# The projections of the mixed input as 16 column pairs of 7 block products each, with staging through DRAM and other fillers in the attention

## The reference

```python
h = rmsnorm(x, norm_mix_g)
proj = h @ w_in                                   # 1024 x 4104
u_pool, q, k, v, f_logit, g_logit = jnp.split(proj, IN_SPLITS, axis=-1)   # 512, 512, 512, 512, 8, 2048
y_pool = pool_mixer(u_pool, pool_w, pool_scale) @ w_pool_out
y_fox = forgetting_attention(q, k, v, f_logit + b_forget) @ w_fox_out     # 8 heads of 64
gates = jax.nn.sigmoid(g_logit + b_gate)
g_pool, g_fox = gates[..., :D], gates[..., D:]
x = x + (g_pool * y_pool + g_fox * y_fox) @ w_out
```

```python
x = x + memory_cross_attention(rmsnorm(x, norm_x_g), rmsnorm(mem, norm_mem_g), w_xq, w_xkv, w_xo)
gu = rmsnorm(x, norm_ffn_g) @ w_ffn_in
x = x + (jax.nn.silu(gu[..., :D_FF]) * gu[..., D_FF:]) @ w_ffn_out
return rmsnorm(x, norm_final_g)
```

## Time and profile before

| | |
|---|---|
| median of 3 runs | 1522.72 us |
| profiled execution | 1521.78 us, of which the span is 1519.9 us |
| PE (matmul) | 1466.1 us busy, 96% of the span |
| DVE | 898.3 us, 59% |
| ACT | 555.7 us, 37% |
| POOL | 377.9 us, 25% |
| DMA | 147.79 MB moved |

### The profile page before, as it was taken

The page is one execution under the profiler, slowest core; times in us unless marked ns, Lnnn a source line. Parts: engine busy times, 40 slices in busy tenths (PEclk is TensorE's granted clock), DMA queues, the critical chain, the costliest instruction groups (busy, mean ns, idle before and its releaser), DMA issues.

```text
span 1519.9 us, 18589 instructions
## 1 busy us (share of the span) xinstructions
PE 1466.1 (96%) x7268; PEld 1211.3 (80%) x7268; DVE 898.3 (59%) x1226; ACT 555.7 (37%) x987; POOL 377.9 (25%) x311
## 2 busy tenths in 40 slices
PE   5999999999999999999999799999999999999996
PEld 5778888788787888888877678888888888887785
DVE  4272522566665423327563866777677776878966
ACT  5224311656654322216451542222222222444344
POOL 4000000000000000105001654444444443448203
PEclk9999999999999999999999899999999999999998
DMA  7333355531110352513210223323332224883333
GB/s 183 54 48 56 72 82 83 98 57 22 49 29 29 73 80 83 222 51 105 67 42 28 111 70 104 105 104 104 104 104 104 104 104 152 304 285 84 104 97 132
DMA packets 103399, 147.79 MB, mean 97 GB/s; under 512 B 4744, under 2 KB 69768, under 8 KB 101904
## 3 DMA queue, kind: packets, MB, share of 16 engines
q1 hardware_dynamic: 94288, 117.72, 30.0%
q0 software_dynamic: 4464, 15.77, 2.9%
q10 hardware_dynamic: 4560, 13.11, 2.2%
HBM read 113.78 MB, written 32.80 MB: 96 GB/s over the span
## 4 chain that ended last, share of the span: by engine, by line
PE 89%; DVE 5%; POOL 2%; DMA 2%; ACT 1%; issue 1%; SPq 0%; POOLq 0%; DVEq 0%; ACTq 0%
PE ps L1553 27%; PE ps L1554 27%; PE ps L1555 27%; PE ps L1803 2%; PE ps L1752 2%; PE ps L1783 1%; DMA w_raw<-in_w_in 1%; DVE t_lo L1054 1%; PE ps L1784 1%; DVE s_lo L1054 1%; POOL w_lo L517 1%; POOL rstd L509 0%; PE ps L1560 0%; PE ps L1995 0%; DVE hf_lo_B L1054 0%
## 5 line engine op out<-in xcount | busy, mean ns | idle before, releaser
L1043 DVE TENSOR_TENSOR w_lo<-w_raw,w_hi 128x1024 fp32r<-128x1024 f32 (+1 forms) x58 | 70.5, 1216 | 232.2 <-ACT w_hi L657 230.3
L1553 PE MATMUL ps<-h_lo,w_hi 128*128 128x512 f32 (+1 forms) x456 | 181.3, 398 | 6.5 <-POOL w_lo L517 4.6
L1555 PE MATMUL ps<-h_hi,w_lo 128*128 128x512 f32 (+1 forms) x456 | 176.8, 388 | 0.0
L1554 PE MATMUL ps<-h_hi,w_hi 128*128 128x512 f32 (+1 forms) x456 | 176.5, 387 | 0.0
L657 ACT ACTIVATE w_hi<-w_raw 128x1024 fp32r<-128x1024 f32 (+1 forms) x66 | 69.4, 1051 | 286.4 <-PE ps L1555 270.7
L1553 PE MATMUL ps<-t_lo,s_hi 128*128 128x512 f32 x308 | 120.2, 390 | 2.3 <-DVE t_lo L1054 1.5
L1555 PE MATMUL ps<-t_hi,s_lo 128*128 128x512 f32 x308 | 119.9, 389 | 0.0
L1554 PE MATMUL ps<-t_hi,s_hi 128*128 128x512 f32 x308 | 119.9, 389 | 0.0
L1553 PEld LDWEIGHTS ps<-h_lo,w_hi 128*128 128x128 f32 x456 | 86.4, 190 | 23.3 <-POOL w_lo L517 4.8
L1555 PEld LDWEIGHTS ps<-h_hi,w_lo 128*128 128x128 f32 x456 | 86.3, 189 | 17.8
L1554 PEld LDWEIGHTS ps<-h_hi,w_hi 128*128 128x128 f32 x456 | 86.6, 190 | 15.5
(11 more groups left out here) (303 smaller groups left out, 3658.8 us busy)
## 6 DMA issues: line engine op xcount, KB each, us to landing
...
```

The source lines that it names most:

```text
L1043: nc.vector.tensor_tensor(w_lo[n % SLOTS][:, 0:w], w_raw[n % RAWS][:, 0:w], w_hi[n % SLOTS][:, 0:w].bitcast(FP32), ALU.subtract).then_inc( ...
L1553: nc.tensor.matmul(dst, w_h, x_l, start=start, stop=False)
L1554: nc.tensor.matmul(dst, w_h, x_h, start=False, stop=False)
L1555: return nc.tensor.matmul(dst, w_l, x_h, start=False, stop=stop)
```

## The change

The 32 column chunks of w_in with 48 matmuls each become 16 column pairs (`PAIR_COL`), each computed by seven products of 12 matmuls, the same scheme as in the FFN. `ORDER1` lists the 112 products: the pairs are, in order, the four pairs of pool gates (0 to 3), the first pair of fox gates, the two of u, two more of fox gates, the two of V, q and k of heads 0 to 3, q and k of heads 4 to 7, and the last pair of fox gates. POOL makes four weight sums for each pair (`front_sum`) and, between those of pair 0 and of pair 1, sixteen sums of the token tiles. The transposes of x are cut into 28 units of four (`front_unit`): the blocks of x for P1 and P2, and then x22, T3, T1, T2 and T4. V is computed with features on the partitions like the rest and transposed back by PE. Results go from one single buffer per block (`c_st`) to DRAM where they are gates, q or k of pairs 1 to 3 or pooled input (d), and are loaded again when they are wanted. The last pair's products P7, P4, P5 and P3 (`DEFER`), the mix, and w_pool_out are the fillers of the attention (`beside`); the q and k of the next pair are no longer computed there, but loaded, rounded and split. The fox output has no gate products left, and reads its gates from DRAM.

On POOL at the start, before: tiles 4 to 7 need four rstds (ms, rstd), and between them stand the last weight splits.

The diff, cut to its core:

```diff
+NF = 16
+PAIR_COL = ([COL_G + 2 * P * i for i in range(4)] + [COL_G + D, 0, 2 * P, COL_G + D + 2 * P, COL_G + D + 4 * P]
+            + [COL_V, COL_V + 2 * P, COL_Q, COL_K, COL_Q + 2 * P, COL_K + 2 * P, COL_G + D + 6 * P])
+GATE_OF = {0: 0, 1: 2, 2: 4, 3: 6, 4: 8, 7: 10, 8: 12, 15: 14}
+U_PAIRS, V_PAIRS, QK0, QK_REST = (5, 6), (9, 10), (11, 12), (13, 14)
+LAST_PAIR = NF - 1
...
+STEADY = (P1, P2, P3, P6, P5, P7, P4)
+STAGE = ([(0, P1), (0, P2), (1, P1), (1, P2)] + [(0, q) for q in (P3, P5, P6, P7, P4)]
+         + [(1, q) for q in (P3, P6, P5, P7, P4)]
+         + [(g, q) for g in range(2, LAST_PAIR) for q in STEADY] + [(LAST_PAIR, q) for q in (P1, P2, P6)])
+DEFER = (P7, P4, P5, P3)
+ORDER1 = STAGE + [(LAST_PAIR, q) for q in DEFER]
...
+RING1 = 6
+LEAD1 = 4
...
+UNITS_AFTER = {0: (8, 9), 1: (10, 11), 2: (12, 13), 3: (14, 15), 4: (16, 17), 5: (18, 19), 6: (20, 21, 22, 23), 7: (24, 25, 26, 27)}
+UNITS_FOR = {P1: 8, P2: 8, P3: 13, P5: 16, P6: 20, P7: 24, P4: 28}
+SPLIT_AT = {2: 0, 6: 1, 9: 2, 13: 3, 17: 4, 21: 5, 25: 6, 29: 7}
...
+            def front_sum(g, i):
...
+                if i == 0:
+                    for half in range(2):
+                        pool.wait_ge(pair_in[g % 2][half], 16 * (g // 2 + 1))
+                    if g:
+                        pool.wait_ge(op_lo, NTH1[g - 1, P7] + 1)
...
+                if i == 3:
+                    nc.gpsimd.tensor_tensor(s1, s2, a11, ALU.add).then_inc(s_sum, 1)
...
+            for t in range(4, T):
+                front_sum(0, t - 4)
+                rstd_of(t)
+            for t in range(4):
+                pool.wait_ge(xn_ready, 4 + t + 1)
+                nc.gpsimd.tensor_tensor(tok_f[:, t, :], x_t[4 + t][:, 0:HALF], x_t[t][:, 0:HALF], ALU.subtract).then_inc(t_sum, 1)
+            nc.gpsimd.memset(f_w[:, :, HEADS:F_ROWS].bitcast(FP32), 0.0).then_inc(consts_set, 1)
+            for t in range(4):
+                pool.wait_ge(unit_done, 12 + t + 1)
+                nc.gpsimd.tensor_tensor(tok_f[:, t, :], x_t[4 + t][:, HALF:], tok_f[:, t, :], ALU.subtract).then_inc(t_sum, 1)
+            for t in range(4):
+                nc.gpsimd.tensor_tensor(x_t[4 + t][:, 0:HALF], x_t[4 + t][:, HALF:], x_t[4 + t][:, 0:HALF], ALU.subtract).then_inc(t_sum, 1)
+            for t in range(4):
+                pool.wait_ge(unit_done, 16 + t + 1)
+                nc.gpsimd.tensor_tensor(tok_f[:, t, :], tok_f[:, t, :], x_t[t][:, HALF:], ALU.subtract).then_inc(t_sum, 1)
...
+            def front_hi_of(n):
+                g, q = ORDER1[n]
+                if n >= RING1:
+                    act.wait_ge(prod_done, n - RING1 + 1)
...
+                    act.wait_ge(s_sum, 4 * g + {P7: 1, P6: 2, P3: 3, P5: 4}[q])
+                nc.scalar.activation(by_k(front_hi[n % RING1]), front_operand(g, q), ACT.Copy).then_inc(op_hi, 1)
...
+                if q == P6:
+                    act.wait_ge(prod_done, n + 1)
+                    if g:
+                        act.wait_ge(f_ev, FEV["C12", g - 1])
+                    nc.scalar.activation(u2_t[:], ps[:, front_bank(g, q), :], ACT.Copy).then_inc(f_copied, 1)
...
+                for u in UNITS_AFTER.get(n, ()):
+                    front_unit_hi(u)
...
+                if n >= 2 and n + LEAD1 < N_FRONT:
+                    front_hi_of(n + LEAD1)
...
+                if 3 <= u < 7:
+                    act.wait_ge(d_in[(u - 3) // 2], 32)
+                    nc.scalar.activation(d_hi[:, u - 3, :], d_lo[:, u - 3, :].bitcast(FP32), ACT.Copy).then_inc(d_hi_ready, 1)
...
+                if 4 <= u < 12:
+                    g, h = divmod(u - 4, 2)
+                    if u < 11:
+                        act.wait_ge(mix_done, u - 3)
...
+                if u < 3 * T and u % T >= 4:
+                    r = u % T - 4
+                    act.wait_ge(qk_in[r % 2], 16 * (2 * p + r // 2 + 1))
+                    qk_hi_of(p + 1, r, qk_st[:, r % 2, :])
...
+            def last_pair(d):
+                dve.wait_ge(prod_done, N_STAGE + d + 1)
+                bank = ps[:, 7, :]
...
+            def pool_gated(v):
+                c, h = divmod(v, 2)
+                if v % 4 < 3:
+                    dve.wait_ge(po_done, 3 * (v // 4) + v % 4 + 1)
+                else:
+                    dve.wait_ge(w_used, C_PO + v // 4 + 1)
+                dve.wait_ge(g_in[v % 2], 16 * (v // 2 + 1))
+                nc.vector.tensor_tensor(za[c][:, half_of(h)], ps[:, 7, :], g_st[:, v % 2, :], ALU.mult).then_inc(za_done, 1)
...
+            def front_product(n, bank, k0, k1):
+                g, q = ORDER1[n]
+                op, first = OPS[q], q not in (P6, P7) and (g, q) != (LAST_PAIR, P3) or (g, q) == (LAST_PAIR, P7)
+                hi, lo = front_hi[n % RING1], front_lo[n % RING1]
+                for k in range(k0, k1):
+                    last = mm3(ps[:, bank, :], hi[:, tile_of(k)], lo[:, tile_of(k)], h_hi[op][:, k, :], h_lo[op][:, k, :],
+                               first and k == 0, k == 3, not first)
+                if k1 == 4:
+                    last.then_inc(prod_done, 1)
...
             def beside(u, part):
-                if u < 3 * T:
-                    qk_group(4 + u // 2, 2 * (u % 2) + part)
-                elif u < 4 * T:
-                    gate_group(u // 2 - 3 * T // 2, 2 * (u % 2) + part)
+                if u < 4:
+                    if part == 0:
+                        pe.wait_ge(op_lo, N_STAGE + u + 1)
+                        if u:
+                            pe.wait_ge(def_ev, u)
+                    front_product(N_STAGE + u, 7, 2 * part, 2 * part + 2)
+                elif u < 12:
+                    g, h = divmod(u - 4, 2)
+                    if part == 0:
+                        pe.wait_ge(lo_ready, C_PW + 1)
+                        pe.wait_ge(d_lo_ready, g + 1)
+                        if u == 4:
+                            pe.wait_ge(def_ev, 4)
+                        else:
+                            pe.wait_ge(mix_lo, u - 4)
+                        last = mm3(ps[:, 7, :], w_hi[C_PW % SLOTS][:, tile_of(g)], w_lo[C_PW % SLOTS][:, tile_of(g)],
+                                   d_hi[:, g, half_of(h)], d_lo[:, g, half_of(h)], True, True)
+                        last.then_inc(mix_done if u < 11 else w_used, 1)
+                elif u < 28:
+                    v = u - 12
+                    c, h = divmod(v, 2)
+                    n = C_PO + c // 2
+                    if part == 0:
+                        pe.wait_ge(lo_ready, n + 1)
+                        if v == 0:
+                            pe.wait_ge(mix_lo, 2 * NG)
+                        else:
+                            pe.wait_ge(za_done, v)
+                    for k in (2 * part, 2 * part + 1):
+                        w = slice(2 * P * k + (c % 2) * P, 2 * P * k + (c % 2 + 1) * P)
+                        last = mm3(ps[:, 7, :], w_hi[n % SLOTS][:, w], w_lo[n % SLOTS][:, w],
+                                   d_hi[:, k, half_of(h)], d_lo[:, k, half_of(h)], k == 0, k == 3)
+                    if part:
+                        last.then_inc(po_done if v % 4 < 3 else w_used, 1)
```

1285 lines of the change are left out of this document (716 added, 569 removed).

## The result

The changed kernel took 1553.04 us, the median of 4 runs (1551.49 to 1555.85), against 1522.39 for the kernel before (4 runs); the ratio is 1.0205, with a 95% interval of 1.0187 to 1.0223. The forecast was 1530, with a range from 1509 to 1543. The direction was right, the size was not: +30.6 us in place of +7 or so.

What follows compares the result with a forecast made beforehand. TensorE (PE), busy 96% of the span, was taken as the bound. Terms -34.8 work, -2.1 first product, +18.8 start, +0.8, +25.7 attention gave +8.3 on 1521.78 us, so 1530, range 1509 to 1543.

Steps and rivals of the forecast that it cites:

- The work off PE, -34.8: Projections and transposes on PE: 192 fewer matmuls take off 43.5 us, 80 more transposes add 8.7, net -34.8 us.
- The first product: Kernel start: the first projection matmul starts at 19.8 us in place of 21.87, winning 2.1 us.
- The steady front "at nothing": Later projection pairs before attention: PE's waits stay hidden and cost nothing; 1 to 5 us if that cover fails.
- The waits of the start, term +18.8: Front before attention: PE's waits and half clock cost 22.0 us against 3.2 before, +18.8; bounds 14 to 32.
- PE by its own work: products 0 to 6 are over at 49: Start of the front: PE finishes products 0 to 6 with units 8 to 19 at 49 us, then transposes two units and waits.
- ACT's block at operand 9: Start: ACT's copy of operand 9 waits for POOL's sum until 57.4 us, holding everything queued behind; some ten idle microseconds.
- Half clock, 1.7 us in the sum: Start, product 7: PE runs at half clock after some ten idle microseconds, adding 1.7 us.
- the first rival: Start and attention: waits are mostly covered, so the kernel gets faster, 1511 us; chance 0.26.
- The attention, -1.5: Attention: 1.5 us shorter, 209.8 us, since 25.7 of the 27.2 us of PE work removed are lost.
- The much slower case, 1548 at a chance of 0.10: Start and attention both cost their upper bounds, +26.7 us, mostly through POOL at 2.28 a sum; 1548 us, chance 0.10.
- the rule that it cites: SBUF: GpSimd and a two-SBUF-input DVE instruction exclude each other; POOL sums of T4 and pair 1 would take 1.28 us.
- no PE gap over 5 us before 75: Start: a sign that the forecast is wrong, where PE would show no gap over 5 us before 75 us.

Runs made afterwards that it cites:

- r2: The changed kernel with the forget steps spread over pairs 2 to 4, one DVE step behind each product, reciprocal in quarters: 1548.4 us.
- r4: On top of r1, PE transposes units 20 to 27 inside products 6 and 7, and forget-weight preparation moves from product 4 to product 9: 1539.1 us.
- r1: The changed kernel with ACT and DVE making operands 9 to 11 behind units 20 to 27, not ahead of them: 1550.1 us.
- r5: The changed kernel with POOL making pair 1's four weight sums between the second and third group of token sums: 1546.9 us.
- r3: The changed kernel with forget-bias buffers of heads 0 and 1 placed over pair 14's raw data, so their loads start earlier: 1546.0 us.

## Why the prediction was wrong in size

The forecast said +8.3 us on the span, and it came out at +31.4. The 23 us between them are 0.9 for the first product, 6.6 in the start, 7.1 in the steady front, 4.1 in the attention and 4.3 in the rest.

- **The work off PE, -34.8: right.** The fox output took 43.6 as forecast, and the steady products stand 2.72 apart.
- **The first product: nearly.** 20.7 for 19.8.
- **The steady front "at nothing": wrong by 7.1 us.** The forget steps were named as what could break the cover and priced at 1 to 5 us, but not put into the sum; they were counted by number and not one by one. One of them, a reciprocal over 1024 columns on 8 partitions, takes 6.54 us, where a multiplication of the same shape takes 1.20; no row for it was looked up. r2 takes 5.9 us off. Another 1.6 us are a wait of PE ahead of the first deferred product, for ACT, of which 0.8 stood in the forecast.
- **The waits of the start, term +18.8: mis-sized, since PE was taken to be early.** From the first product to product 9 it took 61.8 us for 33.2 of work (9 products and 20 units), 28.6 lost where 22.0 were forecast; in r4 it took 47.8. The step that failed is "PE by its own work: products 0 to 6 are over at 49", and with it that POOL's chain and ACT's block at operand 9 cost some ten idle microseconds. The block came as described, but PE was done with product 6 only at 60.65, 11.7 us later than forecast: 0.9 for the first product, 6.6 for products 0, 2 and 6 at half clock, the rest waits, of which 3.55 ahead of product 6. So the block cost about 3 us (r1, r5). In its place stood PE's order: four units behind a product, with two banks for them, are two trips of transpose, ACT copy and DVE low part with nothing beside them, 9.1 us behind product 6 (6.2 in r1, without the block) and 5.0 behind product 7; r4 wins 7.0 by it, and up to 3.4 more with the forget weights out of the way. I had such trips in the sum, but as a tail of POOL's chain.
- **Half clock, 1.7 us in the sum: it cost 8.9 us in the start alone.** Products 0, 2, 6 and 7 took 5.3, 5.2, 4.4 and 5.0 us for 2.72 each. A row of the kernel before has this price: its first FFN product, behind the wait of 5.6 us that I named under the first rival, takes 5.26 us up to the transpose behind it, at a granted clock of 0.50.

```profile
855.63 0.76 PE L1553 MATMUL ps<-hf_lo_B,w_hi 128*128 128x512 f32 x1 [5.58 <-DVE hf_lo_B L1054]
...
860.89 0.85 PE L1995 MATMUL ps<-ident,xn_b 128*128 128x128 f32 x4
```

- **The attention, -1.5: it came out at +2.6.** The shape was right: the emptied units are bound by DVE and ACT, and the filler's 27.2 us were all lost. The sum had no term for the clock, which was 0.75 from 380 to 390 and 0.71 from 410 to 420. The largest miss is the entry: the reduce was forecast 2.5 us late, by a landing of 4.7, the median of all loads. But the first three loads, of 512 KB each, are issued in one row and landed after 6.7, 7.3 and 8.0 us. In the kernel before, the three that are issued together took 12.8 to 15.0, where the single ones took 3.8 to 5.0; they were issued early enough there to be hidden. r3 won 5.6 by moving two of them.
- **The rest: not in the forecast,** 2 to 4 us, cause open.
- **The rivals.** The measured time lies outside all of them. The much slower case, 1548 at a chance of 0.10, came nearest, though it would have had POOL at 2.28 a sum. POOL's token sums took 1.4 to 1.6 us each on average (6.41 for the four of T1, 5.54, 5.49 and 5.47 for those of T2 to T4), between the two values that the prediction weighed. The three sums of pair 1, with DVE idle beside them, took 1.26 to 1.28, as the prediction has them by the rule that it cites, and not the mean of 1.5; T4's, with DVE beside the first of them, took 1.37 each and not 1.28. POOL's sum for operand 9 was 5 us late (62.5 for 57.4) all the same, mostly because POOL waited 4.2 us for PE's transposes, a wait that the forecast of its chain left out. The range ended at 1543 because I let the two bounds stand against each other; the steady front, the clock, the entry and the rest had been put at nothing or near it, each could only cost more, and all of them did.
- **The announced signs.** First product near 20, yes (20.7); w_out later than 601, yes (628). PE idle behind an ACT copy that waited for POOL's third sum, yes, but for 4.6 us at 61.7 and not for 11 from 50 to 61. That is also a sign of being wrong that I had named: no PE gap over 5 us before 75. The attention was 211 to 214 long, and PE's busy share fell to 51 to 76% between 400 and 430 and to 57 to 82% between 560 and 580, as announced. A third stage losing time, the other sign of being wrong, came with the rest.
